# Retention heads turned by VectorE straight from the projection banks, and three memory-key projections moved ahead of the stick sums

## The chip, the core and the metric

The kernel runs on one core of one Trainium2 chip. That core has five engines: TensorE (PE in the profile; its weight loads are PEld), VectorE (DVE), ScalarE (ACT), GpSimd (POOL) and SyncE (SP, which here only issues DMAs). The engines run their own instruction lists in order and meet at semaphores. The metric is device time in microseconds of the whole program. Times come from executions of the same compiled program; one further execution was profiled, and that one is the source of all rows below.

## The reference, cut to what matters

Two networks follow each other on 256 tokens of width 1024. The first (a short convolution mixer, an attention mixer, gated feed-forward layers) is not touched. The second has two layers, each of which does

```
x = x + head_group_mixer(rmsnorm(x))     # stick-breaking heads and retention heads
x = x + memory_cross_attn(rmsnorm(x), rmsnorm(mem))
x = x + peer_ffn(rmsnorm(x))
```

The mixer projects the normed tokens to queries, keys and values of 8 stick-breaking heads of 64 features, and to q, k, v and a gate of 4 retention heads of 128 features. The retention q and k get a rotary turn before they meet:

```
def rotary(x):                       # x: tokens x 128, halves of 64
    x1, x2 = x[:64], x[64:]
    return concat(x1 * cos - x2 * sin, x1 * sin + x2 * cos)
```

Stick-breaking needs, for each head, z = q.k, a soft term log(1 + exp(-|z|)), a reversed running sum of log(1 - sigmoid(z)) over the keys (the "stick sum"), and an exponential. Memory cross-attention needs keys of the memory tokens, which depend on the memory alone.

## The kernel before, in words

Activations lie with features on the 128 partitions and the 256 tokens along the columns, so a retention head is one 128 x 256 tile and the two halves of a head are partitions 0 to 63 and 64 to 127. Weights come in units of 128 x 1024. SP loads a unit into one of four raw slots, ACT rounds it (`high`, L1280), POOL or VectorE subtracts to get the remainder (`low`, L568 or L1776), and PE multiplies three times (L607 to L609) so that the product is as good as float32. Normalising factors are not applied to the input of the mixer but to its output: `scaled_tile` (L2162) multiplies each projection's bank by `inverse_tile`, the per-token factor that L2156 copies from bank 7.

Each of the two layers runs this stage:

- PE projects 4 stick query tiles, 4 stick key tiles, stick values, 8 retention tiles (`r_qk`: 4 q, then 4 k), retention values, 4 gate tiles. `to_sbuf` on PE uses banks 0 to 3 in turn, and from the fifth tile on it waits until the tile four before it has been evacuated. VectorE evacuates all of them in order with L2162 and L2169.
- Early in this stage ACT issues two DMAs on its own queue: the memory tokens (L1486) and `tables_m` (L1487). The latter holds the masks, the cosine and sine tables of the retention turn, the decay factors and, before the change, the 128 x 128 matrix `turn_ret` that swaps the two halves of a head with a sign.
- Between the retention tiles and the retention values VectorE and ACT norm and split the memory (L2193, L1332, L1776), which all memory projections need.
- PE computes z of 8 stick heads into banks 0 to 3 (L1038, L1039), ACT copies them out (L1505) and computes the soft terms in two halves of four heads (L1510 to L1514).
- PE multiplies the eight `r_qk` tiles by `turn_ret` into banks 4 to 7 (L1046). VectorE multiplies these banks by the sine (L2210) and `r_qk` by the cosine (L2213), and adds the two later (L2229).
- PE runs memory-key projections 0 to 3 into banks 0 to 3 (`memory_keys`).
- VectorE combines and masks the soft terms (L2222, L2226), which raises `stick_in` for each head. PE computes the stick sums of heads 0 to 7 in banks 0 to 3 (L1059 to L1061); from head 4 on it waits until VectorE has read the bank of the head four before it (`stick_arg`, L2236). ACT takes exponentials (L1532, L1534), VectorE masks them (L2239).
- PE computes the retention scores (L1068, L1069), memory-key projection 4, and then weighs the stick values (L1078, L1079), for which it waits for the masked sticks (`broken`).

POOL lowers the first 28 units of a layer, then waits for `head_ready` (the end of L2229) and goes on.

Of the kernel before, what the change touches and what calls it, by code (L numbers as in the profile page):

```python
# [20 lines left out]
P = 128  # L21
# [57 lines left out]
MIX_CONSTS = ["ones64", "tri", "causal", "turn_ret"]  # L79
# [64 lines left out]
def two_blocks(nc, io):  # L144
# [6 lines left out]
    with ctx:  # L151
# [183 lines left out]
        inverse_tile = hot[:, 3072:3072 + TOK]  # L335
        q_heads = qk[:, 0:4, :].rearrange("p c (g t) -> p (c g) t", g=2)
# [223 lines left out]
        @block.gpsimd  # L560
        def _(pool):
            T = tallies()
            all_t = list(T.values())

            def low_part(slot):
                col = slice(slot * UNIT, (slot + 1) * UNIT)
                pool.wait_ge(S["high_ready"], T["high_ready"].next())
                pool.tensor_tensor(low[:, col], raw[:, col], high[:, col].bitcast(f32), ALU.subtract)\  # L568
                    .then_inc(S["low_ready"], 1)

            def low_parts(units):
                with repeat(pool, units // SLOTS, all_t, {"high_ready": SLOTS}):
                    for slot in range(SLOTS):
                        low_part(slot)

            T["high_ready"].n = UNITS_1 + SLOTS
            T["head_ready"].n = 5
            for layer in range(LAYERS):

                pool.wait_ge(S["low_ready"], T["high_ready"].value())  # L580
                for slot in range(SLOTS):
                    low_part(slot)
                low_parts(UNITS_H - SLOTS)

                pool.wait_ge(S["head_ready"], T["head_ready"].next(4))
                for slot in range(SLOTS):
                    low_part(slot)
                low_parts(UNITS_POOL - UNITS_H - SLOTS)

                T["high_ready"].next(UNITS_2 - UNITS_POOL)  # L590
# [3 lines left out]
        def _(pe):  # L594
# [398 lines left out]
            for layer in range(LAYERS):  # L993
# [51 lines left out]
                for c in range(4):  # L1045
                    pe.matmul(ps[4 + c][:, :], mix_const("turn_ret"), r_qk[:, 2 * c:2 * c + 2, :], start=True, stop=True)\  # L1046
                        .then_inc(S["head_turned"], 1)
                wait("z_copied", 4)
                for c in range(4):
                    memory_keys(c, c)  # L1050

                for hd in range(SBH):
                    wait("stick_in")
                    if hd >= 4:
                        wait("stick_arg")
                    else:
                        keys_kept(hd)
# [7 lines left out]
                wait("head_ready", 4)  # L1065
                for hd in range(RH):
                    q, k = r_qk[:, hd, :], r_qk[:, 4 + hd, :]
                    pe.matmul(ps[hd][:, 0:TOK], k[:, 0:P], q, start=True, stop=True)  # L1068
                    pe.matmul(ps[hd][:, TOK:SPAN], k[:, P:TOK], q[:, P:TOK], start=True, stop=True)\  # L1069
                        .then_inc(S["ret_scored"], 1)  # L1070
                memory_keys(4, 6)
# [193 lines left out]
        def _(act):  # L1265
# [216 lines left out]
            for layer in range(LAYERS):  # L1482
# [44 lines left out]
                for c in range(4):  # L1527
                    memory_keys(c, c)
                for hd in range(SBH):
# [4 lines left out]
                    act.activation(part, part, ACT.Exp, scale=-1.0).then_inc(S["stick_exp"], 1)  # L1534
                memory_keys(4, 6)
# [183 lines left out]
        def _(dve):  # L1719
# [428 lines left out]
            for layer in range(LAYERS):  # L2148
# [7 lines left out]
                mark(dve.tensor_copy(inverse_tile, ps[7][:, 0:TOK]))  # L2156
                settle()

# [20 lines left out]
                for c in range(4):  # L2179
                    scaled_tile(r_qk[:, c, :], c)  # L2180
                wait("rooted")
                dve.reciprocal(inverse_of[:, 0:2], roots_of[:, 0:2]).then_inc(S["inverted"], 1)
                for c in range(4):
                    scaled_tile(r_qk[:, 4 + c, :], c)
# [22 lines left out]
                wait("mix_loaded", 16)  # L2207
                for c in range(4):
                    wait("head_turned")
                    mark(dve.tensor_tensor(turned[:, c * 512:(c + 1) * 512].rearrange("p (g t) -> p g t", g=2),  # L2210
                                           ps[4 + c][:, :].rearrange("p (g t) -> p g t", g=2),
                                           sin_r.rearrange("p (g t) -> p g t", g=1).to_broadcast([P, 2, TOK]), ALU.mult))
                    mark(dve.tensor_tensor(r_qk[:, 2 * c:2 * c + 2, :], r_qk[:, 2 * c:2 * c + 2, :],  # L2213
                                           cos_r.rearrange("p (g t) -> p g t", g=1).to_broadcast([P, 2, TOK]), ALU.mult))
                settle()

# [10 lines left out]

                for c in range(4):
                    dve.tensor_tensor(r_qk[:, 2 * c:2 * c + 2, :], r_qk[:, 2 * c:2 * c + 2, :],  # L2229
                                      turned[:, c * 512:(c + 1) * 512].rearrange("p (g t) -> p g t", g=2), ALU.add)\  # L2230
                        .then_inc(S["head_ready"], 1)
# [323 lines left out]
def constant_columns():  # L2555
# [10 lines left out]
    for name, half in (("turn_axial", 32), ("turn_ret", 64)):  # L2566
        turn = np.zeros((P, P))
        for c in range(P):
            if c // half % 2 == 0:
                turn[c + half, c] = -1  # L2570
            else:
                turn[c - half, c] = 1
        one[name] = turn
# [8 lines left out]
    for h in range(RH):  # L2582
        log_g = np.log1p(-2.0 ** (-5.0 - h))
        for col, s0, q0, n in ((0, 0, 0, TOK), (TOK, P, P, P)):
# [5 lines left out]
            lay([one[n] for n in MIX_CONSTS] + [np.cos(ret), np.sin(ret), decay.reshape(P, -1)]))  # L2590
# [109 lines left out]
```

## Time and profile before

| what | value |
|---|---|
| runs of the kernel before | 3625.65, 3626.46, 3628.28 us, median 3626.46 us |
| the profiled execution, span from its first to its last instruction | 3626.6 us |
| PE busy in that span | 3567.0 us (98%) |
| VectorE busy | 2605.0 us (72%) |
| ACT busy | 1585.6 us (44%) |
| POOL busy | 1027.3 us (28%) |

The profile gives no time around the span, so the span stands for the profiled execution's own time; it is 0.1 us off the median. The two layers of the second network begin their mixer stage at about 1575 us and 2600 us. In the rows, a line such as "1595.54 0.48 PE L607 ... [0.52 <-DVE sb_k L2162]" has start, duration, engine, source line, operation, what it writes and reads, and in brackets how long the engine had been idle and whose instruction ended that.

### The profile page before, as it was taken

Reading aid. Unit: us, or ns where it says so; the run is one execution under the profiler, and the core shown is the slowest. Engines: PE = TensorE matmul, PEld = TensorE weight load, DVE = VectorE, ACT = ScalarE, POOL = GpSimd, SP = SyncE. Lnnn points to the kernel's source line nnn. Section 1 sums busy time; section 2 is a strip of 40 time slices with the busy share of each in tenths; the row PEclk is TensorE's granted clock in tenths of the full one; section 3 lists DMA queues with packets and bytes.
Section 4 is the critical chain, followed back from the end, with each engine's and each line's share of the span. In section 5 each row is a group of like instructions: output and inputs, shape, how many; then the busy total and the mean of one; then the engine's idle time right before and its main releaser. Section 6 shows DMA issues by size and latency. Waiting matters only on the chain.

```text
span 3626.6 us, 65658 instructions
## 1 busy us (share of the span) xinstructions
PE 3567.0 (98%) x22786; PEld 3275.2 (90%) x22786; DVE 2605.0 (72%) x4691; ACT 1585.6 (44%) x2204; POOL 1027.3 (28%) x436
## 2 busy tenths in 40 slices
PE   9999999999999999999999999999999999999999
PEld 7888888888888879998999999888889999998887
DVE  7868787777873566645478666888644696668887
ACT  3223323223322355556555555444465555554443
POOL 0000000000000000055688877000267687771000
PEclk9999999999999999999999999999999999999999
DMA  7555444554543324663457666777745476666776
GB/s 255 186 169 165 166 138 147 163 191 147 173 151 101 103 70 152 192 218 115 151 189 235 220 220 213 252 255 251 243 145 157 146 240 217 220 224 230 254 252 214
DMA packets 203270, 682.64 MB, mean 188 GB/s; under 512 B 22497, under 2 KB 24673, under 8 KB 193889
## 3 DMA queue, kind: packets, MB, share of 16 engines
q1 hardware_dynamic: 174162, 570.31, 48.6%
q10 hardware_dynamic: 28944, 110.11, 8.7%
q8 instruction: 107, 1.75, 0.2%
q14 instruction: 57, 0.47, 0.0%
HBM read 643.63 MB, written 36.70 MB: 188 GB/s over the span
## 4 chain that ended last, share of the span: by engine, by line
PE 84%; DVE 8%; POOL 2%; issue 2%; DMA 1%; ACT 1%; SPq 0%; POOLq 0%; DVEq 0%; ACTq 0%
PE bank L607 25%; PE bank L608 25%; PE bank L609 25%; POOL low L568 2%; PE bank L1194 2%; PE bank L821 1%; DVE best_p L2331 1%; DVE top_i L2331 1%; DVE low L1776 1%; PE bank L799 1%; DVE best L2327 1%; DVE sums L2396 0%; DVE choice L2402 0%; DVE sums L2399 0%; DMA acts_in<-acts_spill 0%
## 5 line engine op out<-in xcount | busy, mean ns | idle before, releaser
L568 POOL TENSOR_TENSOR low<-raw,high 128x1024 fp32r<-128x1024 f32 x432 | 1027.0, 2382 | 2253.3 <-DVE low L1776 1922.6
L1280 ACT ACTIVATE high<-raw 128x1024 fp32r<-128x1024 f32 x1040 | 1092.1, 1056 | 1234.9 <-PE bank L609 873.3
L607 PE MATMUL bank<-h_lo,high 128*128 128x256 f32 (+1 forms) x4080 | 1250.2, 306 | 9.9 <-DVE h_lo L1853 2.9
L608 PE MATMUL bank<-h_hi,high 128*128 128x256 f32 (+1 forms) x4080 | 1246.0, 305 | 0.0
L609 PE MATMUL bank<-h_hi,low 128*128 128x256 f32 (+1 forms) x4080 | 1246.0, 305 | 0.0
L607 PEld LDWEIGHTS bank<-h_lo,high 128*128 128x128 f32 x4080 | 779.7, 191 | 45.6 <-issue 5.9
L608 PEld LDWEIGHTS bank<-h_hi,high 128*128 128x128 f32 x4080 | 779.7, 191 | 32.7 <-issue 0.7
L609 PEld LDWEIGHTS bank<-h_hi,low 128*128 128x128 f32 x4080 | 779.8, 191 | 32.0
L1776 DVE TENSOR_TENSOR low<-raw,high 128x1024 fp32r<-128x1024 f32 x612 | 732.4, 1218 | 30.7 <-ACT high L1280 29.6
L607 PE MATMUL bank<-low,weighed_hi 128*128 128x512 f32 x1024 | 390.1, 381 | 6.1 <-DVE weighed_lo L1776 6.0
L608 PE MATMUL bank<-high,weighed_hi 128*128 128x512 f32 x1024 | 389.6, 380 | 0.0
L609 PE MATMUL bank<-high,weighed_lo 128*128 128x512 f32 x1024 | 389.2, 380 | 0.0
L1879 DVE CUSTOM_DVE_ANT_0 late_junk<-late_raw,cond_rows 128x1024 f32<-128x1024 f32 x256 | 313.2, 1223 | 6.6
L607 PE MATMUL bank<-up_lo,high 128*128 128x512 f32 (+1 forms) x768 | 273.2, 356 | 3.4 <-DVE low L1776 1.9
L608 PE MATMUL bank<-up_hi,high 128*128 128x512 f32 (+1 forms) x768 | 272.8, 355 | 0.0
L609 PE MATMUL bank<-up_hi,low 128*128 128x512 f32 (+1 forms) x768 | 272.8, 355 | 0.0
L1614 ACT ACTIVATE acts_out<-bank 128x256 f32<-128x256 f32 x256 | 98.5, 385 | 329.3 <-PE bank L609 329.2
L607 PEld LDWEIGHTS bank<-low,weighed_hi 128*128 128x128 f32 x1024 | 194.2, 190 | 35.3 <-DVE weighed_lo L1776 5.4
L609 PEld LDWEIGHTS bank<-high,weighed_lo 128*128 128x128 f32 x1024 | 194.4, 190 | 27.9
L608 PEld LDWEIGHTS bank<-high,weighed_hi 128*128 128x128 f32 x1024 | 194.3, 190 | 27.6
L2443 DVE TENSOR_TENSOR weight_of<-bank,weight_of 128x512 f32 x128 | 88.1, 688 | 150.4 <-ACT weight_of L1650 150.2
L1823 DVE SCALAR_TENSOR_TENSOR x<-bank,mod,x 128x256 f32<-128x256 f32 (+1 forms) x136 | 60.6, 480 | 165.9 <-PE bank L609 164.7
(337 smaller groups left out, 4624.1 us busy)
## 6 DMA issues: line engine op xcount, KB each, us to landing
raw<-in_experts SPq DMA_DIRECT2D x512, 512.0 KB, 3.4
raw<-in_w SPq DMA_DIRECT2D x176, 512.0 KB, 4.2
late_raw<-in_mod_late ACTq DMA_DIRECT2D x64, 1024.0 KB, 4.9
acts_spill<-acts_out ACTq DMA_DIRECT2D x128, 256.0 KB, 2.2
acts_in<-acts_spill SPq DMA_DIRECT2D x128, 256.0 KB, 3.5
raw<-in_w_in SPq DMA_DIRECT2D x56, 512.0 KB, 4.2
raw<-in_w SPq DMA_DIRECT2D x64, 384.0 KB, 3.2
raw<-in_w SPq DMA_DIRECT2D x64, 320.0 KB, 3.6
```

Of the source, the lines that this page charges most:

```text
L568: pool.tensor_tensor(low[:, col], raw[:, col], high[:, col].bitcast(f32), ALU.subtract)\
L607: pe.matmul(out, a[0], b[1], start=start, stop=False, **more)
L608: pe.matmul(out, a[0], b[0], start=False, stop=False, **more)
L609: return pe.matmul(out, a[1], b[0], start=False, stop=stop, **more)
L1194: mm = pe.matmul(out, hot_rows[:, 1 + g % 2, q, :], hot_gated[:, g % 2, q].rearrange("p a n -> p n a"), start=True, stop=True)
L1280: act.activation(high[:, slot * UNIT:(slot + 1) * UNIT], raw[:, slot * UNIT:(slot + 1) * UNIT], ACT.Copy)\
L1614: act.activation(by_halves(acts_out[:, j % 4, :]), unpaired(ps[j % 2][:, 0:TOK]), ACT.Gelu)\
L1776: return dve.tensor_tensor(lo, whole, hi.bitcast(f32), ALU.subtract)
L1823: ins = dve.scalar_tensor_tensor(out=out, in0=bank, scalar=mod[:, bass.ds(j * 2 + col, 1)], in1=old, op0=ALU.mult, op1=ALU.add)
L1879: dve.tensor_tensor_reduce(out=late_junk, in0=late_raw[:, (2 * slot + u) * UNIT:(2 * slot + u + 1) * UNIT], in1=cond_rows[:, stream, :], s ...
L2331: mark(dve.max_index(where(g)[:, lo], values(g)[:, lo], src(g)))
L2443: dve.tensor_tensor(out, sums[:, 1], out, ALU.add).then_inc(S["spread_copied"], 1)
```

## The change: what it does

1. `turn_ret` leaves `tables_m` (2432 columns instead of 2560), the four PE multiplications per layer with it (L1046) go, and so do VectorE's L2210, L2213 and L2229. The sine table is stored with the sign of the turn.
2. VectorE makes two more tiles after `inverse_tile`: the factor times cosine and the factor times sine. It waits for `tables_m` before them, which is ahead of the evacuation of the first stick query tile.
3. `turned_tile` replaces `scaled_tile` for the eight `r_qk` tiles: two multiplications of 64 partitions each read one half of the bank and write the other half of a spare tile, one multiplies the bank in place by the cosine factor, one adds the two into `r_qk`.
4. On PE, memory keys 0 to 2 go right behind z, into banks 4 to 6, and the stick sums follow; memory key 3 (bank 7) moves behind the retention scores. ACT's list has the same order.
5. POOL's second batch waits for `stick_in` of all eight heads.

```diff
-MIX_CONSTS = ["ones64", "tri", "causal", "turn_ret"]
+MIX_CONSTS = ["ones64", "tri", "causal"]
@@ hot tile
+        inverse_cos, inverse_sin = hot[:, 2048:2048 + TOK], hot[:, 2048 + TOK:2048 + 2 * TOK]
+        swapped = hot[:, 2560:2560 + 2 * TOK].rearrange("p (b t) -> p b t", b=2)
@@ POOL
-                pool.wait_ge(S["head_ready"], T["head_ready"].next(4))
+                pool.wait_ge(S["stick_in"], T["stick_in"].next(SBH))
@@ PE
-                for c in range(4):
-                    pe.matmul(ps[4 + c][:, :], mix_const("turn_ret"), r_qk[:, 2 * c:2 * c + 2, :], start=True, stop=True)\
-                        .then_inc(S["head_turned"], 1)
+                for c in range(3):
+                    memory_keys(c, 4 + c)
+
                 wait("z_copied", 4)
-                for c in range(4):
-                    memory_keys(c, c)
-
                 for hd in range(SBH):
                     wait("stick_in")
                     if hd >= 4:
                         wait("stick_arg")
-                    else:
-                        keys_kept(hd)
...
-                wait("head_ready", 4)
                 for hd in range(RH):
...
+                memory_keys(3, 7)
+                keys_kept(2)
                 memory_keys(4, 6)
@@ VectorE
                 mark(dve.tensor_copy(inverse_tile, ps[7][:, 0:TOK]))
+                wait("mix_loaded", 16)
+                for out, table in ((inverse_cos, cos_r), (inverse_sin, sin_r)):
+                    mark(dve.tensor_tensor(out, ps[7][:, 0:TOK], table, ALU.mult))
                 settle()
+                def turned_tile(c):
+                    bank, other = ps[c % 4], swapped[:, c % 2]
+                    wait("unit_used")
+                    for here, there in ((slice(0, 64), slice(64, P)), (slice(64, P), slice(0, 64))):
+                        mark(dve.tensor_tensor(by_halves(other[here, :]), unpaired(bank[there, 0:TOK]),
+                                               by_halves(inverse_sin[there, :]), ALU.mult))
+                    settle()
+                    mark(dve.tensor_tensor(unpaired(bank[:, 0:TOK]), unpaired(bank[:, 0:TOK]), by_halves(inverse_cos), ALU.mult))
+                    settle()
+                    dve.tensor_tensor(by_halves(r_qk[:, c, :]), unpaired(bank[:, 0:TOK]), by_halves(other), ALU.add)\
+                        .then_inc(S["evacuated"], 1)
...
-                wait("mix_loaded", 16)
-                for c in range(4):
-                    wait("head_turned")
-                    mark(dve.tensor_tensor(turned[:, c * 512:(c + 1) * 512].rearrange("p (g t) -> p g t", g=2),
-                                           ps[4 + c][:, :].rearrange("p (g t) -> p g t", g=2),
-                                           sin_r.rearrange("p (g t) -> p g t", g=1).to_broadcast([P, 2, TOK]), ALU.mult))
-                    mark(dve.tensor_tensor(r_qk[:, 2 * c:2 * c + 2, :], r_qk[:, 2 * c:2 * c + 2, :],
-                                           cos_r.rearrange("p (g t) -> p g t", g=1).to_broadcast([P, 2, TOK]), ALU.mult))
...
-                for c in range(4):
-                    dve.tensor_tensor(r_qk[:, 2 * c:2 * c + 2, :], r_qk[:, 2 * c:2 * c + 2, :],
-                                      turned[:, c * 512:(c + 1) * 512].rearrange("p (g t) -> p g t", g=2), ALU.add)\
-                        .then_inc(S["head_ready"], 1)
@@ constants
-            lay([one[n] for n in MIX_CONSTS] + [np.cos(ret), np.sin(ret), decay.reshape(P, -1)]))
+            lay([one[n] for n in MIX_CONSTS] + [np.cos(ret), np.sin(ret) * np.where(i < 64, 1, -1)[:, None], decay.reshape(P, -1)]))
```

## Rows read from the trace of the kernel before

**Rows 1.** Page, busy time by engine; then busy time of one stretch (PE, PEld, DVE, ...).

```profile
PE 3567.0 (98%) x22786; PEld 3275.2 (90%) x22786; DVE 2605.0 (72%) x4691; ACT 1585.6 (44%) x2204; POOL 1027.3 (28%) x436
1584.00:1592.00 8.00, 8.00 (x74) 8.00 (x74) 1.27 (x3) 3.18 (x3) 6.21 (x4) 1.00 0.93 367
```

**Rows 2.** DMA issues by line (us to landing), layer 0, layer 1; issue times.

```profile
tables_m<-in_tables_m ACTq DMA_DIRECT2D x1, 1280.0 KB, 10.1
...
tables_m<-in_tables_m ACTq DMA_DIRECT2D x1, 1280.0 KB, 9.6
...
L1487 ACTq DMA_DIRECT2D tables_m<-in_tables_m x2: 450/958/1467, 1578.8 to 2604.2; - x2
```

**Rows 3.** Timeline of VectorE, first evacuations of layer 0 and of layer 1.

```profile
1582.12 1.08 DVE L2162 TENSOR_TENSOR sb_q<-bank,hot 128x256 f32<-128x256 f32 x3
1584.34 0.42 DVE L2162 TENSOR_TENSOR sb_q<-bank,hot 128x256 f32<-128x256 f32 x1 [1.14 <-PE bank L609]
...
2609.76 0.42 DVE L2162 TENSOR_TENSOR sb_q<-bank,hot 128x256 f32<-128x256 f32 x1 [1.14 <-PE bank L609]
```

**Rows 4.** A PE idle; then busy time of stretches (PEclk is the number after POOL's).

```profile
1848.36 0.33 PE L607 MATMUL bank<-low,p_q_hi 128*128 128x128 f32 x1 [1.92 <-DVE p_q_lo L1776]
...
2594.00:2599.00 5.00, 2.35 (x16) 2.06 (x16) 4.65 (x10) 5.00 (x12) 0.00 (x0) 1.00 0.19 75
1848.90:1855.60 6.70, 6.70 (x34) 6.70 (x33) 6.66 (x32) 2.85 (x5) 1.35 (x1) 0.50 0.47 153
3282.40:3285.70 3.30, 3.30 (x9) 2.60 (x8) 0.30 (x2) 0.00 (x0) 0.00 (x0) 0.50 0.65 200
```

**Rows 5.** Timeline of PE, the turn: layer 0, then layer 1.

```profile
1658.25 5.09 PE L1046 MATMUL bank<-r_qk,tables_m 128*128 128x512 f32 x8
1662.78 0.67 PE L607 MATMUL bank<-mem_lo,high 128*128 128x256 f32 x1
...
2683.26 3.70 PE L1046 MATMUL bank<-r_qk,tables_m 128*128 128x512 f32 x8
2686.40 0.67 PE L607 MATMUL bank<-mem_lo,high 128*128 128x256 f32 x1
```

**Rows 6.** Timeline of PE: stick sum of head 4 and stick values, each layer.

```profile
1677.41 0.60 PE L1059 MATMUL bank<-soft,tables_m 128*128 128x256 f32 x2
...
1687.23 0.66 PE L1078 MATMUL bank<-stick,sb_v 128*64 128x256 f32 x4
...
2701.03 0.60 PE L1059 MATMUL bank<-soft,tables_m 128*128 128x256 f32 x2
...
2711.24 0.66 PE L1078 MATMUL bank<-stick,sb_v 128*64 128x256 f32 x4 [0.31 <-DVE stick L2239]
```

**Rows 7.** Timeline of VectorE, layer 0: soft terms, masks, the removed addition, stick sums.

```profile
1665.48 1.76 DVE L2222 SCALAR_TENSOR_TENSOR soft<-stick,soft 128x1536 f32<-128x1536 f32 x1
1667.27 1.43 DVE L2226 TENSOR_TENSOR soft<-soft,tables_m 128x256 f32<-128x256 f32 x4
...
1671.75 2.49 DVE L2229 TENSOR_TENSOR r_qk<-r_qk,turned 128x512 f32<-128x512 f32 x4
1674.98 0.56 DVE L2236 TENSOR_TENSOR stick<-bank,z 128x384 f32<-128x384 f32 x1 [0.74 <-PE bank L1061]
```

**Rows 8.** Timeline of ACT, last soft term of layer 0 and of layer 1.

```profile
1666.20 1.49 ACT L1514 ACTIVATE soft<-soft 128x1536 f32<-128x1536 f32 x1
...
2691.22 1.49 ACT L1514 ACTIVATE soft<-soft 128x1536 f32<-128x1536 f32 x1
```

**Rows 9.** Timeline of VectorE and POOL at the last retention tile, layer 0.

```profile
1629.48 0.42 DVE L2162 TENSOR_TENSOR r_qk<-bank,hot 128x256 f32<-128x256 f32 x1 [2.25 <-PE bank L609]
...
1630.63 2.37 POOL L568 TENSOR_TENSOR low<-raw,high 128x1024 fp32r<-128x1024 f32 x1 [0.31 <-ACT high L1280]
1630.89 2.38 DVE L1776 TENSOR_TENSOR mem_lo<-mem,mem_hi 128x256 fp32r<-128x256 f32 x1
```

**Rows 10.** One line's instructions, ns min/median/max.

```profile
L2162 DVE TENSOR_TENSOR r_qk<-bank,hot x16: 423/425/425, 1610.7 to 2654.9; 128x256 f32<-128x256 f32 x16
```

More of the change, by code:

```diff
@@ L576, in _ @@
             T["high_ready"].n = UNITS_1 + SLOTS
-            T["head_ready"].n = 5
             for layer in range(LAYERS):
@@ L1525, in memory_values @@
                             .then_inc(S["evacuated"], 1)
-                for c in range(4):
-                    memory_keys(c, c)
+                for c in range(3):
+                    memory_keys(c, 4 + c)
                 for hd in range(SBH):
@@ L1534, in _ @@
                     act.activation(part, part, ACT.Exp, scale=-1.0).then_inc(S["stick_exp"], 1)
+                memory_keys(3, 7)
                 memory_keys(4, 6)
@@ L2179, in _ @@
                 for c in range(4):
-                    scaled_tile(r_qk[:, c, :], c)
+                    turned_tile(c)
                 wait("rooted")
                 dve.reciprocal(inverse_of[:, 0:2], roots_of[:, 0:2]).then_inc(S["inverted"], 1)
-                for c in range(4):
-                    scaled_tile(r_qk[:, 4 + c, :], c)
+                for c in range(4, 8):
+                    turned_tile(c)
                 wait("scale_ready")
@@ L2205, in _ @@
                 mark(dve.tensor_scalar(stick[:, :], z[:, :], 0.0, None, ALU.max))
-                wait("mix_loaded", 16)
-                for c in range(4):
-                    wait("head_turned")
-                    mark(dve.tensor_tensor(turned[:, c * 512:(c + 1) * 512].rearrange("p (g t) -> p g t", g=2),
-                                           ps[4 + c][:, :].rearrange("p (g t) -> p g t", g=2),
-                                           sin_r.rearrange("p (g t) -> p g t", g=1).to_broadcast([P, 2, TOK]), ALU.mult))
-                    mark(dve.tensor_tensor(r_qk[:, 2 * c:2 * c + 2, :], r_qk[:, 2 * c:2 * c + 2, :],
-                                           cos_r.rearrange("p (g t) -> p g t", g=1).to_broadcast([P, 2, TOK]), ALU.mult))
                 settle()
@@ L2226, in _ @@
                         dve.tensor_tensor(diag(soft, hd), diag(soft, hd), mask, ALU.mult).then_inc(S["stick_in"], 1)
-                for c in range(4):
-                    dve.tensor_tensor(r_qk[:, 2 * c:2 * c + 2, :], r_qk[:, 2 * c:2 * c + 2, :],
-                                      turned[:, c * 512:(c + 1) * 512].rearrange("p (g t) -> p g t", g=2), ALU.add)\
-                        .then_inc(S["head_ready"], 1)
                 for hd in range(SBH):
@@ L2565, in constant_columns @@
     }
[L2566 to L2573, printed above, removed]
+    half, turn = 32, np.zeros((P, P))
+    for c in range(P):
+        if c // half % 2 == 0:
+            turn[c + half, c] = -1
+        else:
+            turn[c - half, c] = 1
+    one["turn_axial"] = turn
     f = np.float32
```

## The prediction

> **What bounds the kernel now.** I read the page first: TensorE (PE) is busy for 3567.0 us of 3626.6 [rows 1]. So PE's list is the clock of the program, and an edit counts by what it takes from that list or by the holes that it makes in it. Next I read PE's timeline around the edit, for what it spends on the turn [rows 5] and where it waits behind it [rows 6]. Then VectorE's and ACT's timelines in the same stretch [rows 3, 7 to 9], to see what becomes last once PE has less to do. Last, because the change moves a wait on a DMA to an earlier place, the landing of that DMA [rows 2] beside the stretch in which it would now be waited for [rows 1, 3]. The reader is to see there that PE has no idle time at all between 1584 and 1592 us: whatever stops it there is paid in full.
>
> All sums go against the profiled execution's 3626.6 us. The median of the runs shown is 3626.46 us, 0.1 us away, so nothing has to be converted. A measurement of this kernel tells 0.2% (7.25 us) from no change; the bounds are 3619.2 and 3633.7 us.
>
> **Part 1: the wait for the tables moves ahead of the first evacuation.** ACT issues the load of `tables_m` at 1578.8 us in layer 0 and at 2604.2 in layer 1, and it lands 10.1 and 9.6 us later [rows 2], at 1588.9 and 2613.8. VectorE begins the evacuation of the stick query tiles at 1582.1 and, by the same pattern, finishes the fourth from 2609.8 on [rows 3]. With the change it stands at the wait for the tables from 1582.1, and everything is queued behind it: the two factor tiles and all evacuations. PE may do four projections without an evacuation. The fourth ends when its evacuation begins, at 1584.3 and 2609.8 [rows 3]. The fifth needs bank 0, so PE stands still from there.
>
> When does it go on? The table block loses 128 of 2560 columns, 5%, which is worth between nothing and 5% of 10 us; I take the middle, 0.25 us: 1588.7 and 2613.6. Then come two multiplications of the kind of L2162 (0.33 us from start to start, as three take 1.08; 0.42 for the last), and the first evacuation, 0.42 [rows 3]: 1.2 us, and 0.1 for three semaphores. PE goes on at 1590.0 and 2614.9. The holes are 5.65 and 5.15 us, **10.8 us together**. Nothing gives that back: PE was fully busy there [rows 1], and when it resumes it has at most four prepared weight units, which make no projection faster. The lower end of this term is 0 (tables in time), the upper one 11.6 us (no earlier landing, 0.3 us more for each restart).
>
> **Part 2: the clock behind such a hole.** After an idle of 1.92 us PE ran at a granted clock of 0.50 for 6.7 us from 1848.9 on; another such stretch, from 3282.4, lasted 3.3 us [rows 4]. That is the 1.2 GHz level instead of 2.4. But with 2.65 us of idle spread over 5 us from 2594 on the clock stayed at 1.00 [rows 4]. The holes here are over twice as long in one piece as the one that brought the clock down, so I take it that it falls in both layers. A projection at half clock takes twice as long, so a low stretch of 3.3 to 6.7 us loses 1.7 to 3.4 us. The part of it that lies inside the hole costs nothing. I take 1.9 us each, near the shorter row: **3.8 us**; the ends are 0 and 6.8.
>
> The Trainium skill (TensorE: Matmul & The Clock Gate, section "HAM oscillation — how this bites in real kernels") says that a matmul engine left waiting for a DMA between bursts is throttled to half rate and begins each burst cold. By that rule both holes cost the clock as well, and the sum stays as below; by the 2594 row alone they might not, which is the first rival.
>
> **Part 3: the turn leaves PE, and what is late then.** The eight passes of L1046 take PE from 2683.26 to 2686.40, 3.14 us, in layer 1 and 4.53 us in layer 0 [rows 5]. If PE alone counted, 6.3 to 7.7 us would go. But the stick sums now come behind three memory keys, and one key moves behind the retention scores, so they start sooner and meet VectorE. A projection takes 2.67 us (0.42 and the 2.25 of idle ahead of it [rows 9]), so keys 0 to 2 are done 8.0 us after z, at about 1666.3 and 2691.3. Before, VectorE began to read head 0 at 1674.98 [rows 7] and PE began head 4, three heads further, at 1677.4 [rows 6]: over 0.8 us a head. Four heads bring PE to about 1669.7 and 2694.7. Head 4 needs the bank of head 0, which VectorE frees only after all eight masks. That chain starts at ACT: the last soft term ends at 1667.7 and 2692.7 [rows 8], and nothing moves it. Then come L2222 (1.76 us), four masks (1.43), and L2236 of head 0 (0.56) [rows 7]: 3.75 us. Head 4 starts at 1671.4 and 2696.5 instead of 1677.4 and 2701.0 [rows 6], 6.0 and 4.6 us earlier. The idle ahead of it, at most 1.8 us, is in this. From head 4 to the stick values it was 9.8 and 10.2 us [rows 6]; the second had 0.31 of idle for the masks, which now have a key more to finish in. It is now one key longer: 12.5 and 12.6. Stick values start at 1683.9 and 2709.1: **3.3 and 2.1 us earlier, 5.4 together**. Without VectorE's bound the gain would be the 7.7 us above, and if PE's clock falls before head 4 it is some 2 us. Behind the stick values the order of PE, ACT and VectorE is as before, so the gain is kept.
>
> **Part 4: VectorE's new work.** L2210, L2213 and L2229 go; the last (2.49 us [rows 7]) stood between the masks and the first stick sum, and its absence is in part 3. In exchange each retention tile takes four operations instead of one. The rows have no operation on 64 partitions and none that writes other partitions than it reads. Below, each is 0.33 (start to start); above, 2.38, the longest that a 256-column operation took while POOL ran [rows 9]. I take 0.42, L2162's, the nearest row, as both read a bank and a tile: its maximum over sixteen is 425 ns with POOL at work beside it [rows 10]. A tile is then 0.33 + 0.42 + 0.03 + 0.42 + 0.03 + 0.42 = 1.65 us, under the 2.67 us that PE takes for one. So PE never waits for it, and VectorE, idle for 2.25 of each 2.67, has the room.
>
> Only the last tile could be felt. It ends 1.23 us later, and the memory's norm and split are queued behind it; ACT's rounding and POOL's lowering for the gate tiles wait for those. Here POOL is the cover. VectorE's first `mem_lo` starts at 1630.89 and lasts 2.38 us, until just after POOL's operation has ended at 1633.0 [rows 9]. That POOL operation follows PE's last projection and doesn't move, so a `mem_lo` that comes 1.2 us later still ends at 1633.3. Cost 0; without this cover 1.2 us in each layer.
>
> The POOL batch starts with the eighth mask, 1670.9 instead of 1674.2, no later than PE needs it. Keys 0 to 3 were lowered before, so PE's new place for them waits for nothing. I cost this at 0.
>
> **The sum.** 3626.6 + 10.8 + 3.8 - 5.4 = **3635.8 us**, 9.2 us or 0.25% slower.
>
> **The rivals.**
> - *The clock holds.* Same holes, no low stretch: 3626.6 + 10.8 - 5.4 = 3632.0. For it speaks the 2594 stretch, against it the 1.92 us idle [rows 4].
> - *The tables are in time.* This is the other side. If the tables were loaded when VectorE asks for them, only part 3 would be left: 3626.6 - 5.4 = 3621.2, not slower; with the full 7.7 us, 3618.9. It decides at 1584.3 us less the 1.2 us of restart: a landing by 1583.1 makes no hole. The 10.1 us [rows 2] would have to shrink to 4.3. Both layers show the long landing, and the smaller block changes a quarter of a microsecond.
> - *The sticks give nothing.* The new idle ahead of head 4 brings the clock down there too, in both layers, and takes 3.4 us back: 3639.2. For it: the low stretch after 1.92 us; against it: this idle is 1.8 us at most, and shorter where PE comes late.
> - *Turning across partitions is slow.* At 2.38 us for each of the two half operations a tile takes 5.6 us, PE waits 2.9 us for each of eight tiles, 23 us per layer: 3682. Against it: rows 10; the rows can't exclude it.
>
> **How the numbers follow.** Forecast 0.62, of which I give 0.08 to times just under 3633.7; the clock holds 0.17; tables in time 0.07; sticks give nothing 0.10; slow turning 0.04. Slower by over 0.2%: 0.54 + 0.10 + 0.04 and 0.02 of the second case, 0.70. Faster by over 0.2%: 0.03, the upper part of the third case. Within 0.2%: 0.27. The forecast's own range is 3632 to 3640. To hold 8 in 10 it goes to 3628 (the clock holds and the restart or the sticks give more) and to 3642 (both long low stretches); tables in time and slow turning stay out.
>
> **What would show it.** After the change PE's largest waits should be two at L607 of 5 to 6 us each, ended by VectorE's first evacuation, near 1590 and 2615, with PEclk at 0.5 behind them. VectorE's first factor tile should start as `tables_m` lands. L1046 should be gone, r_qk's evacuations should take four operations in 1.6 to 2.0 us, and head 4 of the stick sums should start 3.8 us after ACT's last soft term. PE's wait for POOL ahead of the gate tiles should be as long as before. I am wrong if PE runs from the fourth to the fifth projection without a hole, or if the hole is there and the total is not slower.

## The result and the profile after

Over five runs each the changed kernel takes 3641.57 us (3637.95 to 3645.28), the kernel before 3626.46 us (3625.65 to 3631.9 over five runs): a ratio of 1.0045, 95% interval 1.0034 to 1.0055. A second set of runs of the same kernel gave 3638.55 us against 3626.05, 1.0033 (1.0020 to 1.0045). So it is 12.5 to 15.1 us slower; 9.2 were forecast. The profiled span grew from 3626.6 to 3639.8 us, 13.2 us.

The page of the changed kernel, busy time by engine (busy us, share of the span, instructions), answers to [rows 1]:

```profile
span 3639.8 us, 65646 instructions
PE 3565.2 (98%) x22770; PEld 3277.7 (90%) x22770; DVE 2609.1 (72%) x4719; ACT 1584.8 (44%) x2204; POOL 1025.5 (28%) x436
```

PE has 16 instructions fewer and 1.8 us less work, yet the span is 13.2 us longer. The time is in waits and in the clock. The view of PE's waits has a line at its head that the kernel before doesn't have (total, times, longest):

```profile
PE bank L608 <- DVE sb_q L2177: 13.3, 2, 8.1
```

PE's and VectorE's timelines show the two places (start, duration, instruction, idle ahead of it and what ended it). The loads of the tables, by line (the last number is us from issue to landing), stand below:

```profile
1590.42 0.75 DVE L2157 TENSOR_TENSOR hot<-bank,tables_m 128x256 f32<-128x256 f32 x2 [9.06 <-DMA tables_m<-in_tables_m]
...
2619.77 0.75 DVE L2157 TENSOR_TENSOR hot<-bank,tables_m 128x256 f32<-128x256 f32 x2 [6.18 <-DMA tables_m<-in_tables_m]
```

```profile
1591.68 0.58 PE L608 MATMUL bank<-h_lo,high 128*128 128x256 f32 x1 [8.11 <-DVE sb_q L2177]
...
2621.04 0.58 PE L608 MATMUL bank<-h_lo,high 128*128 128x256 f32 x1 [5.23 <-DVE sb_q L2177]
```

```profile
tables_m<-in_tables_m ACTq DMA_DIRECT2D x1, 1216.0 KB, 12.3
mem_raw<-in_mem ACTq DMA_DIRECT2D x1, 1024.0 KB, 8.4
...
tables_m<-in_tables_m ACTq DMA_DIRECT2D x1, 1216.0 KB, 9.4
mem_raw<-in_mem ACTq DMA_DIRECT2D x1, 1024.0 KB, 5.6
```

In layer 0 ACT issues the tables at 1578.09 and they land 12.3 us later, at 1590.4; VectorE makes two factor tiles and one evacuation, and PE goes on 1.3 us behind the landing. In [rows 2] the same load had taken 10.1 us. In layer 1 it is 9.4, after 9.6 before.

Busy time in stretches of 2 us around the first hole (PE, PEld, DVE, ACT, POOL busy, then PEclk, DMA share, GB/s):

```profile
1586.00:1588.00 2.00, 0.00 (x0) 0.00 (x0) 0.00 (x0) 0.00 (x0) 1.09 (x1) 1.00 1.00 409
1588.00:1590.00 2.00, 0.00 (x0) 0.00 (x0) 0.00 (x0) 0.00 (x0) 0.00 (x0) 0.74 0.97 364
1590.00:1592.00 2.00, 0.32 (x1) 0.32 (x2) 1.55 (x5) 0.00 (x0) 0.00 (x0) 0.50 0.35 141
1592.00:1594.00 2.00, 2.00 (x11) 2.00 (x11) 0.62 (x2) 0.00 (x0) 0.00 (x0) 0.50 0.02 8
1594.00:1596.00 2.00, 2.00 (x12) 2.00 (x12) 0.00 (x0) 0.00 (x0) 0.00 (x0) 0.56 0.00 0
1596.00:1598.00 2.00, 2.00 (x21) 2.00 (x20) 0.42 (x1) 1.06 (x1) 0.26 (x1) 1.00 0.00 0
```

Two things are to be seen. While PE waits, the 16 DMA engines are full (0.97 to 1.00, 364 to 409 GB/s), so the load that it waits for shares them with others. And the clock falls to 0.50, the 1.2 GHz level, inside the hole and comes back only near 1596: PE issues 11 or 12 products in 2 us instead of 21. Behind the second hole it is the same:

```profile
2622.00:2624.00 2.00, 2.00 (x12) 2.00 (x11) 0.00 (x0) 0.00 (x0) 0.00 (x0) 0.50 0.40 160
2624.00:2626.00 2.00, 2.00 (x11) 2.00 (x11) 0.00 (x0) 0.00 (x0) 0.00 (x0) 0.50 0.03 8
```

The yardstick for all runs below is one stretch of PE, from VectorE's copy of the factor (L2156 before, L2154 after) to PE's first product for the sticks' values, which holds the first eight projections. Its two ends in layer 0, before and then after:

```profile
1581.66 0.42 DVE L2156 COPY hot<-bank 128x256 f32<-128x256 f32 x1 [2.48 <-PE bank L682]
1595.54 0.48 PE L607 MATMUL bank<-low,h_hi 128*128 128x512 f32 x1 [0.52 <-DVE sb_k L2162]
...
1580.93 0.42 DVE L2154 COPY hot<-bank 128x256 f32<-128x256 f32 x1 [2.48 <-PE bank L683]
1605.12 0.48 PE L608 MATMUL bank<-low,h_hi 128*128 128x512 f32 x1 [0.52 <-DVE sb_k L2177]
```

It is 13.88 us in both layers before. After it is 24.19 and 22.02: 10.31 and 8.14 more, 18.45 in all. Of this 13.34 is idle; the other 5.11 is put down to the clock, which run e4 below tests. At the other end of the change, from PE's first z product to the first stick values, it was 34.47 and 33.05 us before and is 31.20 and 31.42 after: 4.9 us gained. The ends of layer 0 that [rows 6] do not show, the first z product before, then after, and the first stick values after:

```profile
1652.76 0.71 PE L1038 MATMUL bank<-sb_q,sb_k 64*128 64x256 f32 x4 [0.52 <-DVE r_g L2162]
...
1662.36 0.71 PE L1039 MATMUL bank<-sb_q,sb_k 64*128 64x256 f32 x4 [0.52 <-DVE r_g L2177]
...
1693.56 0.66 PE L1075 MATMUL bank<-stick,sb_v 128*64 128x256 f32 x4
```

With -0.7 from ahead of the first changed place and +0.4 from the stretches in which nothing was changed, that is the 13.2 us.

VectorE's turn of one tile, layer 0, answers to the estimate of 1.65 us; the second fence is PE's stick sum of head 4 in both layers, the third ACT's last soft term of layer 0 (for [rows 6 and 8]):

```profile
1620.30 0.88 DVE L2166 TENSOR_TENSOR hot<-bank,hot 64x256 f32<-64x256 f32 x2 [3.04 <-PE bank L610]
1621.21 0.43 DVE L2169 TENSOR_TENSOR bank<-bank,hot 128x256 f32<-128x256 f32 x1
1621.68 0.42 DVE L2171 TENSOR_TENSOR r_qk<-bank,hot 128x256 f32<-128x256 f32 x1
```

```profile
1680.98 0.67 PE L1055 MATMUL bank<-soft,tables_m 128*128 128x256 f32 x2
...
2711.27 0.67 PE L1055 MATMUL bank<-soft,tables_m 128*128 128x256 f32 x2 [1.53 <-DVE stick L2237]
```

```profile
1675.62 1.49 ACT L1511 ACTIVATE soft<-soft 128x1536 f32<-128x1536 f32 x1
```

A tile takes 1.80 us of the 2.67 that PE needs, and head 4 starts 3.87 us after ACT's last soft term has ended, in layer 1 too (3.75 forecast).

### The profile page after: what moved, and what is told of

Same layout as the page of the kernel before. It is cut to its first block, busy times and chain, and to the rows that moved or that the text cites. A ratio compares the mean times of both kernels' runs of the same rounds, so it can differ in the third digit from the quotient of the medians.

```text
span 3639.8 us, 65646 instructions
## 1 busy us (share of the span) xinstructions
PE 3565.2 (98%) x22770; PEld 3277.7 (90%) x22770; DVE 2609.1 (72%) x4719; ACT 1584.8 (44%) x2204; POOL 1025.5 (28%) x436
## 4 chain that ended last, share of the span: by engine, by line
PE 84%; DVE 8%; issue 3%; POOL 2%; ACT 1%; DMA 1%; SPq 0%; POOLq 0%; DVEq 0%; ACTq 0%
PE bank L608 25%; PE bank L610 25%; PE bank L609 25%; POOL low L570 2%; PE bank L1191 2%; PE bank L822 1%; DVE best_p L2332 1%; DVE top_i L2332 1%; DVE low L1774 1%; PE bank L800 1%; DVE best L2328 1%; DVE sums L2397 0%; DVE sums L2400 0%; DVE choice L2403 0%; PE bank L709 0%
## 5 line engine op out<-in xcount | busy, mean ns | idle before, releaser
L608 PE MATMUL bank<-h_lo,high 128*128 128x256 f32 (+1 forms) x4080 | 1252.8, 307 | 22.6 <-DVE sb_q L2177 13.3
```

The lines of the kernel that those rows point to most:

```text
L608: pe.matmul(out, a[0], b[1], start=start, stop=False, **more)
```

## Experiments

Theory 1: the loss is the early wait alone, a hole as long as the landing makes it and the half clock behind it; the rest of the change gains some 5 us. The rivals: turning on VectorE or the new order costs by itself; the hole would only move with the wait; what follows the hole is not the clock.

**The wait behind the values (e1), and again in another set of runs (e7).**

```diff
-                wait("mix_loaded", 16)
-                for out, table in ((inverse_cos, cos_r), (inverse_sin, sin_r)):
-                    mark(dve.tensor_tensor(out, ps[7][:, 0:TOK], table, ALU.mult))
                 settle()
...
                 scaled_rows([sb_v[:, s, :] for s in range(2)], 0)
+                wait("mix_loaded", 16)
+                for out, table in ((inverse_cos, cos_r), (inverse_sin, sin_r)):
+                    mark(dve.tensor_tensor(out, ps[7][:, 0:TOK], table, ALU.mult))
+                settle()
                 for c in range(4):
                     turned_tile(c)
```

> The kernel after, with the wait for the tables and the two factor tiles moved from ahead of VectorE's first evacuation to behind the two value tiles of the sticks, just ahead of the first turned tile. Nothing else is changed. Theory 1 (the loss is the early wait: holes of 8.1 and 5.2 us in TensorE's work, and the half clock behind them, 2.2 and 2.9 us): all 18.4 us go, 3641.6 - 18.4 = 3623.2 us, faster than the kernel before by 3 to 5 us; no wait of TensorE for VectorE of over 1 us between the fourth and the fifth projection. If in some execution the tables land as late as 12.3 us after their issue they are still in time, because VectorE now asks for them 13 us or more after the issue. Rival A (the turning on VectorE or the new order costs by itself, and the wait was only where it showed): not below 3632 us. Rival B (TensorE has to wait for the landing wherever the wait stands): a hole moves to the first retention tile and the time stays within 5 us of 3641.6.

> The kernel after with the wait for the tables and the two factor tiles behind the sticks' value tiles, as run before, beside its variants on the same chip. Expected again 3618 to 3624 us, a ratio to before of 0.998 to 0.999; no hole between the fourth and the fifth projection whatever the landing.

Measured: 3619.41 us, ratio 0.9987 (0.9976 to 0.9998), and 3619.68 us, 0.9986 (0.9977 to 0.9995). The stretch is 13.88 us again in both layers of both. VectorE's timeline of e1 shows the four query tiles evacuated at once, and the factor tiles of layer 1 without a wait:

```profile
1580.99 1.08 DVE L2174 TENSOR_TENSOR sb_q<-bank,hot 128x256 f32<-128x256 f32 x3
1583.21 0.42 DVE L2174 TENSOR_TENSOR sb_q<-bank,hot 128x256 f32<-128x256 f32 x1 [1.14 <-PE bank L610]
...
2626.88 0.75 DVE L2193 TENSOR_TENSOR hot<-bank,tables_m 128x256 f32<-128x256 f32 x2
```

The tables landed no sooner in this profile:

```profile
tables_m<-in_tables_m ACTq DMA_DIRECT2D x1, 1216.0 KB, 12.4
```

So a late landing costs nothing where it is asked for late. Both rivals fall, as no hole has moved and the time is far below 3632: the loss was the place of the wait. The stretch gives back the 18.4 us that were expected; in the medians 22.2 us separate this kernel from the changed one in the first set of runs (3641.57 and 3619.41) and 18.9 in the second (3638.55 and 3619.68).

**The wait alone in the kernel before (e2).** The turn stays on PE, the order is the old one.

```diff
                 mark(dve.tensor_copy(inverse_tile, ps[7][:, 0:TOK]))
+                wait("mix_loaded", 16)
                 settle()
...
-                wait("mix_loaded", 16)
                 for c in range(4):
                     wait("head_turned")
```

> The kernel before, whose only change is that VectorE's wait for the tables stands ahead of its first evacuation instead of ahead of the retention heads' turn; the turn stays on TensorE, and the order of memory keys and stick sums is the old one. Theory 1: the loss without the gain. The holes are those of the kernel after less the two factor multiplications (0.7 us each layer), 7.4 and 4.5 us, plus 5.1 us for the clock: 3626.5 + 17.0 = 3643.5 us, over the kernel after. Should the larger table block of this kernel land later, some tenths more. Rival A (the turning and the order cost, not the wait): 3626.5 us, no change. Rival B (the landing of 12.3 us belongs to the smaller table block or to one execution): holes of 4.3 to 5 us in each layer by the landings seen before the change, 10.1 and 9.6 us, thus 3635 to 3638 us.

Measured: 3644.45 us, 1.0054 (1.0041 to 1.0067). PE's holes are these, 13.15 us together:

```profile
1594.44 0.58 PE L607 MATMUL bank<-h_lo,high 128*128 128x256 f32 x1 [6.86 <-DVE sb_q L2163]
...
2624.30 0.58 PE L607 MATMUL bank<-h_lo,high 128*128 128x256 f32 x1 [6.29 <-DVE sb_q L2163]
```

The larger block landed 11.8 and 11.3 us after its issue; the second is 1.8 us later than in the profile after, and so this hole is longer than the 4.5 us expected. The stretch is 22.48 and 22.37 us, 3.9 us more than the holes explain. Moving one wait makes a kernel slower by 18.5 us in the medians (3644.45 and 3625.95) with nothing else changed, where 17.0 were expected: the mechanism needs neither the turning nor the new order, and both rivals of this run fall.

**The tables ahead of the memory in ACT's queue (e3).**

```diff
-                act.dma_start(mem_raw, io["mem"]).then_inc(S["mem_loaded"], 16)
                 act.dma_start(tables_m, io["tables_m"]).then_inc(S["mix_loaded"], 16)
+                act.dma_start(mem_raw, io["mem"]).then_inc(S["mem_loaded"], 16)
```

> The kernel after, with the load of the tables put ahead of the load of the memory rows in ACT's queue; both wait for nothing in between, so the two only change places. Theory 1 (the length of the hole is the landing of the tables, and that is set by what stands ahead of them and beside them): the tables land as the memory did, 8.4 and 5.6 us after their issue, 3.9 and 3.8 us earlier; the holes shrink to 4.2 and 1.4 us and the clock falls behind the first at most: 3641.6 - 7.7 - 2.9 = 3631 us, 3628 to 3636. Rival (the two loads share the same DMA engines all the way and land together): no change, 3640 to 3643. A second thing to see: the memory rows land 4 us later, and their squares are asked for behind the stick value tiles, so a later wait there would give back part of the gain.

Measured: 3630.64 us, 1.0010 (1.0001 to 1.0020). The loads by line, layer 0 then layer 1, and PE's holes:

```profile
tables_m<-in_tables_m ACTq DMA_DIRECT2D x1, 1216.0 KB, 7.5
mem_raw<-in_mem ACTq DMA_DIRECT2D x1, 1024.0 KB, 10.9
...
tables_m<-in_tables_m ACTq DMA_DIRECT2D x1, 1216.0 KB, 8.4
mem_raw<-in_mem ACTq DMA_DIRECT2D x1, 1024.0 KB, 11.8
```

```profile
1590.14 0.38 PE L608 MATMUL bank<-h_lo,high 128*128 128x256 f32 x1 [2.91 <-DVE sb_q L2177]
...
2618.36 0.58 PE L608 MATMUL bank<-h_lo,high 128*128 128x256 f32 x1 [3.87 <-DVE sb_q L2177]
```

The tables come 4.8 us sooner in layer 0 and 1.0 in layer 1, the holes are 6.8 us in all instead of 13.3, and the memory, now later, is not missed. Against expectation the second hole is 3.87 us long instead of 1.4 and still brings the clock down: the stretch is 4.79 and 5.63 us too long, 3.6 more than the holes. The profiled execution (3637.43 us) was the slowest of the twelve, 6.8 us above their median, so its holes need not be the usual ones.

**Idle products in the hole (e4).**

```diff
+                        if u == 4:
+                            stay_busy(fill, 5)
                         pe.wait_ge(S["evacuated"], T["evacuated"].at(first + u - 3))
...
-                to_sbuf(8, h, TOK, between=between_first, ready=tile_scaled)
+                to_sbuf(8, h, TOK, between=between_first, ready=tile_scaled, fill=(30, 20)[layer])
```

> The kernel after, with 30 (layer 0) and 20 (layer 1) idle products of a constant tile put on TensorE ahead of its wait for the fifth projection's bank, at 0.23 us each 6.8 and 4.6 us, so that TensorE is busy through most of the hole. The hole's end is VectorE's and doesn't move. Theory 1 (behind the hole the clock is at half, and that costs 2.2 and 2.9 us beyond the hole itself): the clock stays at 1.0 behind the hole, 3641.6 - 5.1 = 3636.5 us, 3635 to 3638. Rival (the slow stretch behind the hole is a cold start of the weights' stream or of VectorE's chain, not of the clock): no change, 3640 to 3643, with the fifth projection as slow as in the kernel after. If the tables land earlier than in the profile of the kernel after, the idle products themselves hold TensorE, and the time is longer by that.

Measured: 3639.58 us, 1.0037 (1.0024 to 1.0050). That misses the 3635 to 3638 us expected, and in the time alone it can't be told from the changed kernel's (the rival had 3640 to 3643); on the clock the trace decides. Its timeline of PE in layer 0, and its busy time in the stretches that answer to those above:

```profile
1587.39 6.86 PE L654 MATMUL bank<-consts 128*128 128x128 f32 x60
...
1594.50 0.38 PE L608 MATMUL bank<-h_lo,high 128*128 128x256 f32 x1 [0.25 <-DVE sb_q L2179]
```

```profile
1592.00:1594.00 2.00, 2.00 (x21) 2.00 (x19) 0.76 (x2) 0.00 (x0) 0.00 (x0) 1.00 0.92 296
1594.00:1596.00 2.00, 1.75 (x16) 1.56 (x15) 1.42 (x4) 0.00 (x0) 0.00 (x0) 1.00 0.35 141
1596.00:1598.00 2.00, 2.00 (x20) 2.00 (x20) 0.42 (x1) 0.52 (x1) 0.00 (x0) 1.00 0.03 8
```

The granted clock stays at 1.00 through the whole hole and behind it. The stretch is 7.21 and 6.35 us too long; the products and the idle left behind them (30 at 0.23 and 0.25 us; 20 at 0.23 and 1.63 us) make 7.1 and 6.2 (a product shows as two records, so 30 are x60). So the part beyond the hole, 5.1 us in the changed kernel, is 0.2 us here: it was the clock. The span (3638.7 us) shows little of it because this execution was 4.0 us behind the changed kernel's before anything differs: VectorE's copy stands at 1584.91 instead of 1580.93. Against the second profile of the changed kernel (e6, copy at 1584.08, span 3638.9) the stretch is 5.4 us shorter in all, and 3.7 us are lost again in the two long stretches that no edit touches, behind the stick values of either layer. Whether the other executions lost it in the same way isn't shown.

**The changed kernel once more (e6).**

> The kernel after, unchanged, for a second profiled execution. Theory 1 with a landing that differs from one execution to the next: in the five profiles so far with the load order of the change's kernel the tables land 10.1, 12.3, 12.4, 11.8 and 11.1 us after their issue in layer 0 and 9.4 to 11.3 in layer 1. The hole should end 1.2 us behind whatever landing this profile shows, in both layers, within 0.2 us; the time 3636 to 3645 us, between 0.2 and 0.6% over before. Rival (the 12.3 us of layer 0 belong to the changed kernel): again 12 us and more in layer 0 and 9.4 in layer 1.

Measured: 3638.55 us, 1.0033 (1.0020 to 1.0045). The landings are 12.2 and 9.6 us, and the holes follow them:

```profile
1594.71 0.58 PE L608 MATMUL bank<-h_lo,high 128*128 128x256 f32 x1 [7.99 <-DVE sb_q L2177]
...
2623.50 0.58 PE L608 MATMUL bank<-h_lo,high 128*128 128x256 f32 x1 [5.43 <-DVE sb_q L2177]
```

This looks like the rival of that run, a landing of 12 us that belongs to the changed kernel. But e7, with the same block and the same loads, shows 9.7 us in layer 0, and e5 and e8 show 11.0 and 12.5 in layer 1. Over the nine profiles that load the memory first, the tables land after 10.1, 12.3, 12.2, 11.8, 11.1, 12.4, 9.7, 12.3 and 12.7 us in layer 0 (median 12.2) and after 9.4 to 12.5 in layer 1 (median 9.7). In layer 0 they land 4.2 to 4.5 us behind the memory each time, so what varies there is already in the memory's landing. What shares the engines can be read from the DMA queues, from the issue of the memory's load to the landing of the tables (packets, MB, share of the 16 engines; q1 has SP's weight loads, q10 ACT's two loads). In layer 0 before, 10.47 us at 391 GB/s, and after, 12.68 us at 379 GB/s:

```profile
q10 hardware_dynamic: 288, 2.36, 55.9%
q1 hardware_dynamic: 471, 1.72, 43.3%
...
q1 hardware_dynamic: 686, 2.49, 51.2%
q10 hardware_dynamic: 288, 2.29, 44.9%
```

The engines are about as fast in both; the later landing has more of the weights moved beside it. In layer 1 that goes with the issue times: in the six profiles where the tables land after 9.4 to 10.3 us, SP issues its next weight load 2.0 us behind the memory's, in the three with 11.0 to 12.5 us 1.2 to 1.4 us behind it. In layer 0 this time is 0.65 to 0.67 us in all nine, and the landing still spreads from 9.7 to 12.7 us. No run changed the weight loads, so the cause of the spread stays open.

**The old order of the keys (e8) and a fourth key ahead of the sticks (e5).** Both stand on e1.

```diff
 # e8, on PE (ACT's list alike)
-                for c in range(3):
-                    memory_keys(c, 4 + c)
                 wait("z_copied", 4)
+                for c in range(4):
+                    memory_keys(c, c)
...
-                memory_keys(3, 7)
-                keys_kept(2)
                 memory_keys(4, 6)
 # e5, on PE (ACT's list alike)
-                for c in range(3):
+                for c in range(4):
                     memory_keys(c, 4 + c)
...
-                memory_keys(3, 7)
                 keys_kept(2)
```

> As the kernel with the late wait, but the four memory keys stand where they stood before the change: behind z in banks 0 to 3, key 4 behind the retention scores, none between z and its copies. The turn is still on VectorE. It tells the two halves of the gain apart. Theory 1 (the gain at the sticks comes from the chain ACT's last soft term, masks, head 0, head 4, which no longer has VectorE's rotation in it; the order of the keys only chooses what lies beside it): after the removal TensorE has 3.1 to 4.5 us less to do and the keys still cover the wait for the soft terms; the four keys need 10.7 us and the first copies of z 1 to 2 us ahead of them, so head 0 starts some 12 us behind z, head 4 some 1.5 us behind what the late-wait kernel shows, but with one key less behind it (2.67 us): 0 to 1.2 us a layer faster than the late-wait kernel, less up to 2 us a layer for TensorE's new idle between z and the first key: within 3 us of the late-wait kernel, 3617 to 3624. Rival (the gain is the new order's): the time of the kernel before, 3626 us.

> As the kernel with the late wait, but four memory keys instead of three stand ahead of the stick sums, in banks 4 to 7, and only the fifth behind the retention scores. Theory 1 (head 4 is bound by VectorE's chain behind ACT's last soft term, and TensorE idles 1.5 us ahead of it in each layer): the fourth key fills that idle, head 4 starts 1.2 us later and one key of 2.67 us is gone behind it: 1.5 us a layer, 3 us in all, faster than the late-wait kernel: 3615 to 3620 us. Rival (TensorE, not VectorE, is last at head 4): no change against the late-wait kernel.

Measured: e8 3619.95 us, 0.9984 (0.9975 to 0.9993); e5 3620.09 us, 0.9983 (0.9974 to 0.9992). From PE's first z product to the first stick values, layer 0 and layer 1:

| kernel | us |
|---|---|
| before | 34.47, 33.05 |
| before with the wait moved (e2) | 33.04, 34.59 |
| after, two profiles | 31.20, 31.42; 31.19, 30.65 |
| late wait (e1, e7) | 31.23, 30.96; 31.33, 31.12 |
| late wait, old order (e8) | 30.11, 29.59 |
| late wait, four keys (e5) | 29.98, 29.44 |

An idle of 1.5 us ahead of head 4 is in ten of the twelve layers profiled with three keys ahead, and in none with four. So the gain comes with the turn leaving this stretch (PE's passes and VectorE's operations together, which no run separates), not from the new order, which gives back 1.3 us a layer of it; the rival of e8 falls, and in this stretch that of e5.

The two layers of an old kernel differ by 1.4 and 1.5 us, and that goes with the clock: behind the wait for ACT's copies of z it falls to 0.50 (before, 1658 to 1660) or 0.52 (e2, 2700 to 2702) in the longer layer and stays at 1.00 in the other. It falls in layer 0 after (0.50 from 1668 to 1670) and in layer 0 of e4 as well. But these are the two layers without the idle ahead of head 4, and they are no longer than the others (31.20 and 31.37 us): there the half clock cost nothing, as PE would have stood idle for VectorE.

In the whole time the 2.6 us of the two layers don't show against e7 (3619.68), so the 3 us expected of e5 are not confirmed there. The profiles of e5 and e8 have more of the half clock in other places (from 2590 to 2596 us the granted clock is 0.77 and 0.75, in e7 1.00), and the stretch behind layer 1's stick values, which no edit touches, takes 915.7 and 915.6 us in them, 913.9 and 913.7 in e1 and e7. Whether that is the order's doing or chance stays open. Three versions, e1, e5 and e8, beat both kernels, the one before by 0.13 to 0.17%, some 5 to 6 us.

## Why the prediction was right or wrong

**Right: the mechanism and the side.** PE's two largest new waits are at the fifth projection, ended by VectorE's first evacuation, and VectorE starts as the tables land; e1 and e2 show that this wait is the loss, with and without the rest of the change. The clock does fall behind both holes, so the rival "the clock holds" (3632.0) is out. So is "the tables are in time": they landed after 12.3 and 9.4 us, where it needed 4.3.

**Wrong: the size, and it is two steps.** The measured median is 5.8 us above the forecast and 1.6 above its own range of 3632 to 3640; the second set's 3638.55 is inside, and both are inside the wider 3628 to 3642. In the pair of profiled spans it is 4.0: 2.5 in the holes, 1.3 in the clock, 0.5 less gained at the sticks, less 0.3 elsewhere; the other 1.8 is the base (below). In the prediction's own terms:

| term | forecast | profile after | second profile |
|---|---|---|---|
| hole, layer 0 | 5.65 | 8.11 | 7.99 |
| hole, layer 1 | 5.15 | 5.23 | 5.43 |
| clock, two layers | 3.8 | 5.1 | 5.5 |
| gain at the sticks | -5.4 | -4.9 | -5.7 |

The step that failed is "When does it go on?" in part 1: the landing of the tables in layer 0 was taken from one profiled execution as if it were a constant, 10.1 us less 0.25 for the smaller block. It is 12.3 and 12.2 us in the two profiles of the changed kernel, and 10.1 is one of the two lowest of nine. Nobody waited for this DMA before the change, so nothing in the old time spoke of its spread. The upper end of that term, 11.6 us (11.9 by its own terms, twice 0.25 and twice 0.3 over the 10.8), let the landing be no later than in that one profile, so the range inherited the error; the holes measured 13.3 and 13.4 us. Layer 1, where the landing was nearly that of [rows 2], came out to 0.1 us, and that is in part luck, with landings from 9.4 to 12.5 us there over the nine. What 5% fewer bytes were worth can't be seen in this spread.

The second step is part 2's price. Taken near the shorter row of [rows 4], 1.9 us each; measured 2.2, 2.9, 3.1 and 2.4, between that value and the long row's 3.4. The four together with e4, where the stretch beyond the hole shrinks to 0.2 us, show that the term is what it was said to be and only its size was off. The Trainium skill (TensorE: Matmul & The Clock Gate, section "HAM oscillation — how this bites in real kernels") has the matmul engine throttled behind a DMA wait and cold at the start of the next burst; the traces agree for the holes of 8.1 and 5.2 us after, 8.0 and 5.4 in e6 and 3.9 in e3 (0.50 behind each).

**Right: part 3.** The chain from ACT's last soft term to head 4 took 3.87 us for 3.75. Layer by layer the gain was 3.27 and 1.63 us for 3.3 and 2.1, and over the eight stretches of the table with the changed order against the four of the old kernels it is 2.65 us a layer, 5.3 for the 5.4 forecast. The rival "the sticks give nothing" is out: behind the 1.53 us of idle ahead of head 4 in layer 1 the granted clock is 1.00. That the gain would shrink to 2 us if the clock fell ahead of head 4 was not borne out: it fell in layer 0 of both kernels, and 3.27 us were gained there.

**Right in effect: part 4.** A tile took 1.80 us, not 1.65. The two half operations take 0.88 us, twice 0.44, and do not overlap as three whole ones do in [rows 3]. The Trainium skill (VectorE: DVE Perf Modes, section "Two Vector instructions with no wait between them") holds back an instruction whose input or output starts in another quadrant of partitions than the last one's in the same memory, until all earlier ones have finished; the row of 0.88 us agrees. PE needs 2.67 us a tile, so nothing waited. The cover at the end held: the first `mem_lo` took 1.13 us instead of 2.38 and ended 0.27 us behind POOL's operation, as before, and PE's wait for POOL ahead of the gate tiles is 1.05 us against 1.03. The rival "slow turning" is out.

**Wrong, at no cost to the forecast: the base.** The prediction compared the profiled span of 3626.6 us with a median of run times and found nothing to convert. In the executions whose span is known the time stands about 1.8 us above it (3641.57 and 3639.8; 3618.65 and 3616.9). So the profiled execution of before was, by that, one of about 3628.4 us, 1.9 us above the median, and the span and the median agreed by luck. The difference of 9.2 us added to the median gives 3635.7 us, the same forecast. But the profiled pair, 13.2 us apart, then understates the 15.1 us between the medians by these 1.9.

## What to carry to other kernels

When a change moves a wait on a DMA to an earlier place, the price is a landing that nobody waited for until now: one profile gives one sample of it, so look at what shares the DMA engines in that stretch and let the range cover more than that sample. Put the consumer behind work that needs nothing from the load; here eight evacuations and one value pair later was free, with landings up to 12.7 us. Add to each hole of PE what the clock takes behind it, which was a quarter to two thirds of the hole here.

## What the runs showed of the hardware

- A load of 1.2 to 1.3 MB, issued at the same place of ACT's list, landed after 9.4 to 12.7 us over nine profiles, with the DMA engines full ahead of the landing (after, 364 to 409 GB/s). Two loads of one queue changed places and landings: the tables took 7.5 us instead of 12.3, the memory 10.9 instead of 8.4 (layer 0, e3 and after). The Trainium skill (DMA: Bandwidth & Descriptors, section "Issuing engines are not separate DMA queues") says that loads started by different engines run on the same 16 DMA engines and interleave; the trace agrees, with 44.9% of the 16 engines for ACT's queue and 51.2% for SP's in the same 12.7 us.
- A hole of 2.91 us (e3) cost 1.9 us of clock behind it, close to the 2.2 behind one of 8.1 us (after); one of 8.0 us cost 3.1 (e6). Products that nobody needs held the clock through 7 us (e4, 1.00 throughout). The length of an idle alone did not tell: one of 1.56 us ahead of the second z products was followed by 0.50 (after, layer 0), one of 1.83 us in the same place by 1.00 (layer 1).
- VectorE writes its result into the other half of the partitions at no extra cost but the lost overlap, 0.44 us for 64 x 256.
- Executions of one and the same program differ by up to 17 us here (kernel before, 3619.9 to 3637.2 us in 23 runs). The profiles reach VectorE's first factor copy between 1580.3 and 1584.9 us, ahead of any change.
